# Adding the sink terms of an attention branch on VectorE in PSUM instead of by TensorE products

## The reference

```python
def sink_softmax(s, sink):
    m = jnp.maximum(jnp.max(s, axis=-1, keepdims=True), sink)
    e = jnp.exp(s - m)
    return e / (jnp.sum(e, axis=-1, keepdims=True) + jnp.exp(sink - m))
```

## Time and profile before

| | |
|---|---|
| time, median of 3 runs | 3153.26 us (3152.05 to 3154.89) |
| span of the profiled execution | 3149.0 us (a time of its own beside that span was not recorded) |
| PE busy | 3040.6 us, 97% of the span |
| PEld busy | 2396.5 us, 76% |
| DVE busy | 1827.3 us, 58% |
| ACT busy | 1296.0 us, 41% |
| POOL busy | 263.8 us, 8% |
| mean granted clock of PE | 0.996 of full speed |

### The profile page before, as it was taken

How to read it: one execution, slowest core, us unless ns; L and a number is a source line. 1 busy time by engine, 2 the same in 40 slices (tenths; PEclk the granted TensorE clock), 3 DMA queues, 4 the chain that set the end, 5 groups by cost and what they waited for, 6 DMA issues and landing times.

```text
span 3149.0 us, 37117 instructions
## 1 busy us (share of the span) xinstructions
PE 3040.6 (97%) x14862; PEld 2396.5 (76%) x14862; DVE 1827.3 (58%) x2911; ACT 1296.0 (41%) x2007; POOL 263.8 (8%) x206
## 2 busy tenths in 40 slices
PE   8999999999999998999999999999999999999998
PEld 4878877877788676767777777788887876788887
DVE  5877675255435767685454786666436662566632
ACT  3244523135532344534454474322225667422222
POOL 0011100001100001102110031000003210000000
PEclk9999999999999999999999999999999999999999
DMA  5222132320012322222112233333332310233332
GB/s 207 73 68 74 48 103 94 109 86 27 21 34 77 104 81 80 67 81 69 51 51 74 83 97 94 94 94 94 95 96 87 114 38 1 78 96 95 94 94 74
DMA packets 78732, 251.52 MB, mean 80 GB/s; under 512 B 9120, under 2 KB 11168, under 8 KB 78560
## 3 DMA queue, kind: packets, MB, share of 16 engines
q1 hardware_dynamic: 72672, 227.91, 22.9%
q0 software_dynamic: 5024, 18.09, 1.8%
q10 hardware_dynamic: 864, 3.15, 0.3%
HBM read 247.01 MB, written 2.10 MB: 79 GB/s over the span
## 4 chain that ended last, share of the span: by engine, by line
PE 46%; ACT 4%; DVE 3%; issue 1%; DMA 0%; POOL 0%; DVEq 0%; ACTq 0%
PE PS L1158 31%; PE PS L1796 4%; PE PS L2816 3%; PE PS L2917 1%; PE PS L1920 1%; PE PS L2894 1%; ACT WH L1107 1%; PE PS L2895 1%; PE PS L2876 0%; PE PS L2838 0%; PE PS L2877 0%; ACT L1982 0%; PE PS L2544 0%; ACT L1984 0%; PE PS L2886 0%
## 5 line engine op out<-in xcount | busy, mean ns | idle before, releaser
L1117 DVE TENSOR_TENSOR WL<-RAW,WH 128x1024 fp32r<-128x1024 f32 (+3 forms) x374 | 423.7, 1134 | 527.2 <-ACT WH L1107 526.5
L1107 ACT ACTIVATE WH<-RAW 128x1024 fp32r<-128x1024 f32 (+3 forms) x397 | 384.6, 972 | 434.7 <-PE PS L1158 331.0
L1796 PE MATMUL PS<-Hh,WH 128*128 128x512 f32 x1376 | 524.4, 381 | 14.8 <-DVE WL L1117 8.2
L1796 PE MATMUL PS<-Hl,WH 128*128 128x512 f32 x1376 | 486.7, 354 | 0.0
L1796 PE MATMUL PS<-Hh,WL 128*128 128x512 f32 x1376 | 485.6, 353 | 0.0
L1796 PEld LDWEIGHTS PS<-Hh,WH 128*128 128x128 f32 x1376 | 259.6, 189 | 74.6 <-issue 22.7
L1158 PE MATMUL PS<-XH,WH 128*128 128x512 f32 x768 | 305.0, 397 | 0.0
L1158 PE MATMUL PS<-XH,WL 128*128 128x512 f32 x768 | 303.4, 395 | 0.0
L1158 PE MATMUL PS<-XL,WH 128*128 128x512 f32 x768 | 303.3, 395 | 0.0
L1796 PEld LDWEIGHTS PS<-Hl,WH 128*128 128x128 f32 x1376 | 259.8, 189 | 47.6 <-issue 10.1
L1796 PEld LDWEIGHTS PS<-Hh,WL 128*128 128x128 f32 x1376 | 260.1, 189 | 40.2
(11 more groups left out here) (404 smaller groups left out, 5740.3 us busy)
## 6 DMA issues: line engine op xcount, KB each, us to landing
RAW<-in_w_in SPq DMA_DIRECT2D x124, 512.0 KB, 3.6
RAW<-in_ffn_in SPq DMA_DIRECT2D x96, 512.0 KB, 3.6
RAW<-in_ffn_out SPq DMA_DIRECT2D x48, 512.0 KB, 3.6
RAW<-in_w_ada SPq DMA_DIRECT2D x32, 384.0 KB, 3.7
RAW<-in_nsa_in SPq DMA_DIRECT2D x21, 512.0 KB, 3.4
RAW<-in_lru_in SPq DMA_DIRECT2D x20, 512.0 KB, 3.5
MW<-in_w_ada SPq DMA_DIRECT2D x32, 256.0 KB, 9.7
BS<-in_bs POOLq DMA_DIRECT2D x16, 512.0 KB, 3.9
```

Source lines behind the costliest of these rows:

```text
L1107: act.activation(WH[half[j]][:, 0:n], RAW[j % NRAW][:, 0:n], ACT.Copy).then_inc(*did("act_whi", ("whi", j)))
L1117: dve.tensor_tensor(WL[half[j]][:, 0:n], RAW[j % NRAW][:, 0:n], WH[half[j]][:, 0:n].bitcast(F32), ALU.subtract).then_inc(*did("dve_wlo", ( ...
L1796: mm = pe.matmul(ps[:, c:c + w_], wt[:, 128 * k:128 * k + 128], x[:, a:a + w_], start=(k == 0 and q == 0), stop=(k == n - 1 and q == 2))
```

## The change

The transposes of the maxima give 64 equal rows instead of one in this branch. ScalarE takes the Exp of the sink from those PSUM rows directly behind the copy of the row, for 64 rows. The sink products and the unit "es" are gone; at "sink" VectorE adds `ER` to the denominators in PSUM, as soon as the last value product and the Exp are done, and `act_fin` waits for that. The maxima are rounded as they are written, so that the row and the sink see the same number.

```diff
@@ branch, used()
-                if i == 1 and br:
-                    out.append(("es", L, br, p, f))
                 if i == 1:
                     out.append(None)
@@ attn, kind "tr"
-                B.release(u, ("row",) + u[1:])
+                B.release(u, ("row",) + u[1:], ("es",) + u[1:] if br else None)
@@ pe_attn
-                elif u[0] == "sink":
-                    pe_sink(pe, L, br, u)
@@ pe_rows
-                mm = pe.transpose(B.of(u)[0:1, 128 * i:128 * i + 128], NM[:, 32 * f + t_:32 * f + t_ + 1], ident)
+                top = NM[:, 32 * f + t_:32 * f + t_ + 1]
+                if br:
+                    mm = pe.transpose(B.of(u)[0:64, 128 * i:128 * i + 128], top.broadcast_to([128, 64]), ident)
+                else:
+                    mm = pe.transpose(B.of(u)[0:1, 128 * i:128 * i + 128], top, ident)
@@ pe_mix_values
-                end = (i == 1 if ctx_q else k == last and i == len(parts[k]) - 1) and not br
+                end = i == 1 if ctx_q else k == last and i == len(parts[k]) - 1
@@ pe_sink
-        def pe_sink(pe, L, br, u):
-            p, f = u[3:]
-            pick = CO[:, 192:320] if slot(br, p, f) else CO[:, 256:384]
-            for half, (a0, n, c) in enumerate(RX[L]):
-                for w in due("pe", [("es", L, br, p, f, h) for h in range(2 if L == 0 else 1)], ("co",)):
-                    pe.wait_ge(*w)
-                mm = pe.matmul(out_bank(L, f)[:, a0:a0 + n], pick, ER[L][half][:, 0:n], start=False, stop=True)
-            mm.then_inc(*did("pe_pv", ("sk",) + u[1:]))
@@ act_rows; act_sink is gone
             act.activation(row, B.of(u)[0:1, 0:n], ACT.Copy, scale=-1.0).then_inc(*did("act_row", ("row",) + u[1:]))
-                act.activation(ER[L][half][64:65, 0:n], row.bitcast(F32), ACT.Exp, bias=sm(f"sink{L}", 2 * p + f, 1)[64:65, :]).then_inc(*did("act_row", ("es", L, br, p, f, half)))
+            if br:
+                for w in due("act", ("sk", L, br, p, 0) if f else ("sk", L, br, p - 1, 1) if p else ("attn", L, br)):
                     act.wait_ge(*w)
+                act.activation(ER[L][half][0:64, 0:n], B.of(u)[0:64, 0:n], ACT.Exp, bias=sm(f"sink{L}", 2 * p + f, 1)[0:64, :], scale=-1.0).then_inc(*did("act_row", ("es",) + u[1:]))
@@ dve_attn
+                elif u[0] == "sink":
+                    p, f = u[3:]
+                    den = sums(L, br, u)[0]
+                    for half, (a0, n, c) in enumerate(RX[L]):
+                        for w in due("dve", ("pv", L, br, p, f, len(score_parts(L, br)) - 1), ("es", L, br, p, f, half)):
+                            dve.wait_ge(*w)
+                        dve.tensor_tensor(den[:, a0:a0 + n], den[:, a0:a0 + n], ER[L][half][0:64, 0:n], ALU.add).then_inc(*did("dve_sk", ("sk", L, br, p, f)))
@@ dve_max
-                dve.scalar_tensor_tensor(mx[:, 0:4], mx[:, 0:4], sm(f"sink{L}", 2 * p + f, 1), mx[:, 8:12], ALU.max, ALU.max)...
+                dve.scalar_tensor_tensor(mx[:, 0:4].bitcast(F32R), mx[:, 0:4], sm(f"sink{L}", 2 * p + f, 1), mx[:, 8:12], ALU.max, ALU.max)...
...
@@ pool_attn
-            for e in ER[L][0:2 - L] if br else ():
-                pool.memset(e[:, :], 0.0).then_inc(*did("pool_set", ("ez", L)))
```

More of the change, by code:

```diff
@@ L1986, in act_attn @@
                     act_rows(act, L, br, u, B)
-                elif u[0] == "es":
-                    act_sink(act, L, br, u)
                 elif u[0] == "fin":
@@ L2057, in act_rows @@
             act.activation(row, B.of(u)[0:1, 0:n], ACT.Copy, scale=-1.0).then_inc(*did("act_row", ("row",) + u[1:]))
-        def act_sink(act, L, br, u):
-            p, f = u[3:]
-            before = ("sk", L, br, p, 0) if f else ("sk", L, br, p - 1, 1) if p else ("ez", L)
-            for half, (a0, n, c) in enumerate(RX[L]):
-                row = QB[L, br][64:65, f, a0:a0 + n]
-                for w in due("act", ("row", L, br, p, f, half), before):
+            if br:
+                for w in due("act", ("sk", L, br, p, 0) if f else ("sk", L, br, p - 1, 1) if p else ("attn", L, br)):
                     act.wait_ge(*w)
-                act.activation(ER[L][half][64:65, 0:n], row.bitcast(F32), ACT.Exp, bias=sm(f"sink{L}", 2 * p + f, 1)[64:65, :]).then_inc(*did("act_row", ("es", L, br, p, f, half)))
+                act.activation(ER[L][half][0:64, 0:n], B.of(u)[0:64, 0:n], ACT.Exp, bias=sm(f"sink{L}", 2 * p + f, 1)[0:64, :], scale=-1.0).then_inc(*did("act_row", ("es",) + u[1:]))
         def sums(L, br, u):
@@ L2217, in dve_max @@
                     dve.wait_ge(*w)
-                dve.scalar_tensor_tensor(mx[:, 0:4], mx[:, 0:4], sm(f"sink{L}", 2 * p + f, 1), mx[:, 8:12], ALU.max, ALU.max).then_inc(*did("dve_mx", ("mxs", L, br, p, f, 0)))
+                dve.scalar_tensor_tensor(mx[:, 0:4].bitcast(F32R), mx[:, 0:4], sm(f"sink{L}", 2 * p + f, 1), mx[:, 8:12], ALU.max, ALU.max).then_inc(*did("dve_mx", ("mxs", L, br, p, f, 0)))
             elif t_ == 4:
@@ L2223, in dve_max @@
                         dve.wait_ge(*w)
-                    dve.tensor_scalar(mx[:, 4:6], mx[:, 4:6], sm(f"sink{L}", 2 * p + f, 1), None, ALU.max).then_inc(*did("dve_mx", ("mxs", L, br, p, f, 1)))
+                    dve.tensor_scalar(mx[:, 4:6].bitcast(F32R), mx[:, 4:6], sm(f"sink{L}", 2 * p + f, 1), None, ALU.max).then_inc(*did("dve_mx", ("mxs", L, br, p, f, 1)))
             else:
```

## The result

The change makes the kernel slower by more than forecast: 3190.06 us median (3184.56 to 3190.75, 4 runs) against 3154.07 us (3152.05 to 3157.72, 4 runs) for the kernel before, ratio 1.0109, interval 1.0098 to 1.0121. The forecast was 3175 us, the range 3150 to 3185. The profiled execution after has a span of 3182.7 us, 33.7 more than before, and a mean clock of 0.991; its own time, 3184.56 us, is the lowest of the four, whose other three show a mean clock of 0.987.

The account below looks back on a forecast made before the run. TensorE, busy 97%, was taken as the bound except at short waits ended by ScalarE or VectorE. Head terms +7.2, +4.4, +2.0 and -1.6 made +12.0 us, the clock +10, giving 3175 us; range 3150 to 3185.

Parts of the forecast that it names:

- first kind: Three heads where VectorE's add stands behind four pairs of normalization instructions: Ln late, together +7.2 us.
- about 46: TensorE's idle time in us forecast for the second branch's two stretches, up from 17.
- Seven of my gaps are longer than 3.1 us: Clock term: TensorE waits in both layers' second branch, each bringing 3.4 us at half rate, 1.4 us lost each: +10 us.
- the bound of eight: Upper bound of the clock term: eight clock drops at 1.7 us each, 13.6 us.
- the sum of +22: Whole forecast change against the profiled execution: +12.0 us without the clock and +10 us for the clock.
- four kinds: The branch's sixteen heads, sorted by their waits: +7.2, +4.4, +2.0 and -1.6, together +12.0 us without the clock.
- the pair of sink Exps: ScalarE's Exp of both halves behind the first layer's row copies: 0.85 us overlapped, bounds 0.8 to 1.2.
- the last head of the first layer: Head followed by work that waits for nothing, so the removed product's time is gained: -1.3 us.
- second and third kinds: Six heads where the Exp delays later exponentials, +4.4 us; three where TensorE waits for the row itself, +2.0 us.
- Rival (b): Add finds VectorE free and Ln is never late: faster, 3145 us, 3136 if all sixteen heads gain; chance 0.12.
- Rival (d): Exp out of PSUM costs like from SBUF, pair at 1.2, clock falls at an eighth place: 3181 us; chance 0.07.

Follow-up runs that it names:

- e4: Kernel before with the sink products left out (no sink term in the denominators), the sink's Exp staying where it was: 3139.6 us, ratio 0.9951.
- e9: Kernel before with the sink product in one fp32r pass contracted over all 128 rows: 3146.7 us, ratio 0.9970.
- e10: Kernel before with only the row transposes widened to 64 equal rows and the maxima rounded: 3154.0 us, ratio 0.9997.
- e8: Kernel before without the unit "es", the same Exp issued behind the exponential of the head's second score part: 3156.0 us, ratio 1.0002.
- e6: Changed kernel with 37 useless filler products in seven groups, meant for seven of TensorE's long waits: 3178.2 us, ratio 1.0073.
- e11: Kernel before with the second branch's seven groups of filler products (26 products) taken out: 3163.3 us, ratio 1.0025.
- e1: Changed kernel with VectorE's add left out and Ln waiting for the last value product alone: 3151.6 us, ratio 0.9988.
- e2: Changed kernel with VectorE's add issued at the last value product, ahead of the last maxima and normalization pairs: 3158.3 us, ratio 1.0011.
- e5: Changed kernel with the add issued early and the sink's Exp computed for each layer's first head only: 3147.4 us, ratio 0.9977.
- e3: Changed kernel, add still late, with the sink's Exp computed for each layer's first head only: 3174.3 us, ratio 1.0063.

## Why the prediction was wrong

**What held.** The removed products were worth 1.30 and 0.86 us a head (e4: -15 of 17.3 us, e9). The add took 0.70 us at 64x512 and 0.42 at 64x256. Ln was released by the add at 14 of 16 heads. The three heads of the first kind went as written: waits of 4.41, 3.73 and 3.71 us against 4.7, 4.2 and 4.2. The rows were waited for 3.14 us twice, against 3.2 and 3.3. Wide transposes and the new spacing cost nothing (e10, e8). TensorE's idle time in the two stretches came to 48 us against "about 46". So the mechanism was right; what failed is above all the size of one term.

**The step that failed: "Seven of my gaps are longer than 3.1 us ... so I take 1.4 each: +10 us. Bounds: nothing, and 8 x 1.7 = 13.6."** The runs showed 10 and 14 periods, which lost 15.8 and 21.8 us of work.

One period for each long gap was nearly right: the kernel after has eight new gaps of over 3 us (4.41, 3.75, 3.77 and 3.52 in the first layer; 3.14, 3.73, 3.71 and 3.14 in the second), and in each profile seven of the eight have a slow period at their end. What the count left out are the others. Behind some of the gaps stand two periods, twice in the first profile and four times in the second. And the clock also fell where I had no gap above 3.1 us: in both profiles after the wait of 2.0 us at the branch's end (921 and 923 us), which the prediction took for none, in the second also after the gap of 3.03 us that the kernel before has too, with a slow period of its own (1500 us), and near 691 us, behind gaps of 0.88 and 0.35. That is 7 + 2 + 1 = 10 and 7 + 4 + 3 = 14, so the bound of eight was wrong as well. The discount from 1.7 to 1.4 us was right in its direction, since part of a slow period falls into the wait, but too large: 1.58 and 1.56 us were measured. With 21.8 us in the term's place the sum is 12.0 + 21.8 = +33.8 us, 3187 us. Of the 11.7 and 17.6 us by which the two spans exceed the sum of +22, this term is 5.8 and 11.8, the waits are 2.3, and of the last 3.5 us most lie outside the branch, as the accounts say.

e6 and e11 show that the clock's part is caused by the gaps and not by something else in the change: filling six of them took 10 to 12 us off the changed kernel, although one more group of fillers stood where nothing waited, and emptying seven in the kernel before added 9. The Trainium skill (TensorE: Matmul & The Clock Gate, Part 1) says that the window of activity is free-running; 10 and 14 periods with equal waits agree with it. I had drawn from it only that some drops could be missing, and not that more could come. No run tells why some gaps bring two periods and some none.

**Smaller terms.** Net of the products the idle time grew by 14.3 us, against +12.0 in the four kinds. Missing were: the pair of sink Exps, taken at 0.85 us overlapped, which measured 1.15 (682 and 469 ns) as they alternate with the copies (the upper bound was 1.2), so the two longest waits for the first exponentials are 3.75 and 3.77 us, not 3.4; the second half of a row 0.71 us later wherever TensorE waits for it (3.52 us at first-layer (3,0), against 2.4); and the last head of the first layer, taken at -1.3 since its successor "waits for nothing". The kernel after, the first product behind the branch's end, and what VectorE and ScalarE did ahead of it:

```profile
919.91 2.69 DVE L2131 TENSOR_TENSOR Gl<-O,Gh 128x768 fp32r<-128x768 f32 x3 [3.19 <-ACT Gh L1995]
...
919.03 3.04 ACT L1995 ACTIVATE Gh<-O 128x768 fp32r<-128x768 f32 x4 [5.28 <-POOL O L2276]
...
920.97 0.63 PE L1794 MATMUL PS<-Gh,WH 128*128 128x512 f32 x1 [1.99 <-issue]
```

It reads Gh and Gl, which hang on the head's own output through GpSimd, so what TensorE gains by then turns into waiting (2.0 us; 1.7 in e1 and e4, which have no add; 0.4 in the kernel before). The profile puts no name to that wait; that it is Gl is argued from the rows and was not tried apart.

**Where my shares were off.** I gave the late add 7.2 us of its own and mixed it with the Exp in the second and third kinds. e2 shows that with the add early the loss falls from 36 to 4 us: 16 us less idle time and 8 to 12 fewer periods. The Exp is worth 11 us with Ln in time (e5) and 14 to 16 with Ln late (e3). Apart, the early add and the single Exp take off 32 and 16 us, together 43, so most of each is its own, where I had expected of e2 only 12 to 18. Rival (b), "the add finds VectorE free", would have needed more than that: e2 gives it free passage and is still 0.1% slower than before, as nearly all of the 17 us from TensorE come back as waits (22.7 + 9.8 us idle in place of 8.6 + 7.7), in the first layer 7.8 us more for ScalarE and 5.1 for VectorE. Rival (d) was nearest to the number, and for a part of the right reason.

## What to carry to other kernels

An instruction moved to an in-order engine waits for all that is written ahead of it there, and everything behind its consumer waits too; read from the timeline what that engine does at that place before pricing the instruction itself (0.70 us of add cost some 30 us, and one line's move took them back). Price the idle time that a change makes on TensorE at more than its length: here 31.6 us of it cost 16 to 22 us more by half-rate work, and the clock's part can be larger than the net of the rest. And before a dear product is moved off a busy engine, see whether it can be made cheap where it is: one pass over full rows took it from 1.30 to 0.36 us and gave the fastest version that leaves nothing out, 0.30% below before (0.18 to 0.42%), with the sink's exponentials rounded to fp32r.

## What the runs showed of the hardware

- The same kernel with the same waits had 10 slow periods in one execution and 14 in another, a difference of 6 us of work in 3188; outside the branch, from 1730 us to 15 us before the end, there are from 2 to 5 of them, from kernel to kernel, where the work is the same.
- A gap's length alone doesn't tell: the gap of 3.03 us that ends at 1496 us in the first profile after, and at 1498 in the second, has a full clock behind it in the first and 0.83 over the next ten microseconds in the second.
- A product that contracts one row among products of 128 rows costs about 0.09 us at each step of start, four steps for a pair of them, 0.36 us in all; with full rows of zeros it costs nothing above its columns.
- Exp out of PSUM took 682 ns for 64x512 and 469 for 64x256, where the exponential of 128x512 out of PSUM took 597; the two with the bias tile SMA (that from SBUF took 717) are slower than the one without, whatever they read; no run changed the bias alone.
